# Two fused blocks on one core: attention weights normalised before they are turned, half the queries per level, another order at one join

## The reference

```python
PHASES = ["na", "ffn", "ple", "da", "ffn", "ple", "glu", "mix", "glu", "ple"]
```

```python
# gated linear recurrence, 4 heads of 128, in chunks of 64
scores = einsum('bhtd,bhsd,bhtsd->bhts', q_c, k_c, exp(b_t - b_s))   # t >= s
o = scores @ v_c + (q_c * exp(b)) @ state
# latent attention, 4 heads, blocks of 128 queries over the causal prefix
pr = softmax(where(mask, q @ k.T * scale, -inf))
o_mla = pr @ v
h = h + concatenate([rms_norm(o_hg) * silu(hg), o_mla]) @ w_out
```

## Time and profile before

| what | value |
|---|---|
| median of 3 runs | 1193.83 us (1193.71 to 1195.09) |
| the profiled execution | 1193.79 us, its span 1191.9 us |
| TensorE matmuls busy | 1179.1 us, 99% of the span, 6915 records |
| TensorE weight loads busy | 1028.1 us, 86% |
| VectorE busy | 933.1 us, 78% |
| ScalarE busy | 665.0 us, 56% |
| GpSimd busy | 139.0 us, 12% |
| mean granted clock of TensorE | 0.998 of full speed |
| DMA | 215.83 MB, 181 GB/s on the mean |

### The profile page before, as it was taken

How to read it: one execution, slowest core, us unless ns; L and a number is a source line. 1 busy time by engine, 2 the same in 40 slices (tenths; PEclk the granted TensorE clock), 3 DMA queues, 4 the chain that set the end, 5 groups by cost and what they waited for, 6 DMA issues and landing times.

```text
span 1191.9 us, 17766 instructions
## 1 busy us (share of the span) xinstructions
PE 1179.1 (99%) x6915; PEld 1028.1 (86%) x6915; DVE 933.1 (78%) x1270; ACT 665.0 (56%) x1059; POOL 139.0 (12%) x265
## 2 busy tenths in 40 slices
PE   8999999999999999999999999999999999999997
PEld 7998988888889989888888988888898888888886
DVE  6866898898777689989888898766776878766765
ACT  6756644444867786544446745444586664444445
POOL 5300600000300011000003100000206410000002
PEclk9999999999999999999999999999999999999999
DMA  9758376655544345665555575556455147556540
GB/s 297 223 156 269 124 244 207 210 179 178 190 139 148 129 163 195 212 205 185 182 173 179 184 230 189 189 187 203 136 191 177 44 161 228 176 197 204 185 142 36
DMA packets 151671, 215.83 MB, mean 181 GB/s; under 512 B 7002, under 2 KB 116956, under 8 KB 151588
## 3 DMA queue, kind: packets, MB, share of 16 engines
q1 hardware_dynamic: 148124, 207.46, 53.1%
q0 software_dynamic: 1760, 3.94, 1.3%
q10 hardware_dynamic: 1704, 3.28, 0.9%
HBM read 213.60 MB, written 1.06 MB: 180 GB/s over the span
## 4 chain that ended last, share of the span: by engine, by line
PE 93%; DVE 3%; ACT 1%; DMA 1%; issue 1%; POOL 0%; SPq 0%; POOLq 0%; ACTq 0%; DVEq 0%
PE work L2491 25%; PE work L2494 13%; PE acc L2072 10%; PE acc L2073 10%; PE acc L2074 10%; PE work L2072 5%; PE work L2073 5%; PE work L2074 5%; PE work L2094 1%; PE work L2480 1%; PE work L2468 1%; DVE w_lo L1357 1%; PE work L2482 1%; PE work L2619 1%; PE acc L2129 1%; PE acc L2270 1%
## 5 line engine op out<-in xcount | busy, mean ns | idle before, releaser
L1357 DVE TENSOR_TENSOR w_lo<-raw,w_hi 128x2048 fp32r<-128x2048 f32 (+1 forms) x192 | 436.0, 2277 | 51.5 <-ACT w_hi L752 51.5
L752 ACT ACTIVATE w_hi<-raw 128x2048 fp32r<-128x2048 f32 (+1 forms) x192 | 363.5, 1899 | 69.0 <-PE work L2494 59.4
L2491 PE MATMUL work<-hT_both,w_hi 128*128 128x512 f32 x1280 | 318.8, 391 | 0.0
L2491 PEld LDWEIGHTS work<-hT_both,w_hi 128*128 128x128 f32 x1280 | 234.8, 188 | 45.1
L2494 PEld LDWEIGHTS work<-hT_both,w_lo 128*128 128x128 f32 x1280 | 174.6, 190 | 12.5
L2494 PE MATMUL work<-hT_both,w_lo 128*128 128x256 f32 x1280 | 178.5, 282 | 0.0
L2072 PE MATMUL acc<-w_hi,aux_hi 128*128 128x512 f32 x400 | 158.0, 395 | 0.0
L2073 PE MATMUL acc<-w_lo,aux_hi 128*128 128x512 f32 x400 | 156.7, 392 | 0.0
L2074 PE MATMUL acc<-w_hi,aux_lo 128*128 128x512 f32 x400 | 155.8, 390 | 0.0
L1131 ACT ACTIVATE aux_hi<-Z 128x256 fp32r<-128x256 f32 x88 | 36.9, 419 | 195.4 <-DVE Z L1780 107.4
L1751 DVE TENSOR_REDUCE Z<-work 128x256 f32<-128x512 f32 x88 | 60.6, 689 | 89.5 <-PE work L2494 87.8
(11 more groups left out here) (283 smaller groups left out, 1740.2 us busy)
## 6 DMA issues: line engine op xcount, KB each, us to landing
raw<-in_ffn_w_in SPq DMA_DIRECT2D x44, 1024.0 KB, 5.1
raw<-in_ffn_w_out SPq DMA_DIRECT2D x22, 1024.0 KB, 5.1
raw<-in_w_gate SPq DMA_DIRECT2D x22, 1024.0 KB, 5.3
raw<-in_w_up SPq DMA_DIRECT2D x22, 1024.0 KB, 5.3
raw<-in_w_down SPq DMA_DIRECT2D x22, 1024.0 KB, 4.9
raw<-in_da_w_qkv SPq DMA_DIRECT2D x12, 1024.0 KB, 5.3
raw<-in_na_w_qkv SPq DMA_DIRECT2D x10, 1024.0 KB, 7.3
raw<-in_ple_w_gate SPq DMA_DIRECT2D x8, 1024.0 KB, 5.2
```

What stands on the lines that cost most here:

```text
L752: act.activation(w_hi[:, n % RING, 0:size], raw[:, n % RAW, 0:size], ACT.Copy).then_inc(hi_done, 1)
L1357: dve.tensor_tensor(w_lo[:, n % RING, 0:size], raw[:, n % RAW, 0:size], w_hi[:, n % RING, 0:size].bitcast(F32), ALU.subtract).then_inc(lo_ ...
L2491: pe.matmul(b.rearrange("p (e s) -> p e s", e=2), v[0][:, k, cols(c % 2)], hT_both[:, k, :, :], start=k == 0, stop=False)
```

## The change

It has three parts.

1. **Normalised weights, moving over resting values.** VectorE multiplies the exponentials by the reciprocal of their row sums before TensorE turns them (`normalised7`, with a semaphore of its own, `w7_ready`). In `outputs` the values are now the stationary operand and the turned weights the moving one, in two matmuls of 256 and 128 columns, so the result has queries along the free axis, as `late_piece` needs it. The stage `omla` with its eight transposes is gone. ScalarE and VectorE split each head's result directly (`output7` on both).
2. **Order in the mixer.** `gate_piece(1, 0)` stands directly after `gate_piece(0, 0)`, ahead of `weights(2)`. ScalarE's queue has `exps7(3)`, `output7(0)` and `output7(1)` ahead of `weights_turned7(2)`, and `output7(2)`, the slab and `output7(3)` between `decay(1)` and `decay(2)`. In levels 1 to 4 the moving operand holds only the 64 queries of the late halves, and `gather` writes only those.
3. **The join of phases 2 and 3.** TensorE's `turn_x(3, 0)` stands between the two halves of the last gate piece, `turn_x(3, 1)` ahead of the last block of `value_rows(3, 0, 1, 0)`. ScalarE and VectorE take their slab earlier, and their splits, sums and additions are interleaved in another order.

```diff
@@ plan @@
-                stage(f"V7.{u}", 1)
-            stage("omla", 2, (0, 1))
+                stage(f"V7.{u}", 1, (0,))
@@ ScalarE, gated_end, ph == 2 @@
                     gates(2, 1)
+                    feed(b + 6)
                     pre(3, 0)
-                    feed(b + 6)
                     gates(2, 2)
                     gates(2, 3)
-                    tile_parts(3, 0, range(4))
+                    tile_parts(3, 0, range(2))
+                    pre(3, 1, (0,))
+                    tile_parts(3, 0, range(2, 4))
+                    pre(3, 1, (1,))
                     gates(2, 4)
                     tile_parts(3, 0, range(4, 6))
-                    pre(3, 1, (0, 1))
+                    pre(3, 1, (2,))
                     tile_parts(3, 0, range(6, 8))
-                    pre(3, 1, (2,))
                     feed(b + 7)
                     tile_parts(3, 1)
@@ ScalarE, mixer @@
+            def output7(u):
+                g = G[f"V7.{u}"]
+                full(act, g)
+                split(aux_hi[:, u, :], backwards(bank(g)[:, 0:S]))
...
                 exps7(2)
+                exps7(3)
+                output7(0)
+                output7(1)
                 weights_turned7(2)
-                exps7(3)
                 weights_turned7(3)
                 decay(1)
+                output7(2)
                 feed(b + 15)
+                output7(3)
                 decay(2)
-                for t in range(T):
-                    full(act, G["omla"] + t)
-                    split(aux_hi[:, :, t * P:(t + 1) * P], backwards(bank(G["omla"] + t, 4)))
                 decay(3)
@@ VectorE, gated_end, ph == 2 @@
                     add_gated(2, 1)
+                    feed(b + 6)
                     normed(3, 0)
-                    feed(b + 6)
-                    tile_parts(3, 0, range(4))
                     add_gated(2, 2)
                     add_gated(2, 3)
-                    tile_parts(3, 0, range(4, 6))
+                    tile_parts(3, 0, range(4))
                     add_gated(2, 4)
-                    tile_parts(3, 0, range(6, 8))
+                    tile_parts(3, 0, range(4, 8))
                     normed(3, 1)
@@ VectorE, mixer @@
-            def output7(u):
+            def normalised7(u):
                 dve.wait_ge(exp_done, exps_before(7) + 2 * (u + 1))
                 link(dve.reciprocal(rinv[:, u % 4, 0:2], rsum[:, u % 4, 0:2]))
...
+                    tile = sc7[:, u, seen[a]]
+                    ins = dve.tensor_scalar(tile, tile, rinv[:, u % 4, a:a + 1], None, ALU.mult)
+                ins.then_inc(w7_ready, 1)
...
+            def output7(u):
+                split(aux_lo[:, u, :], backwards(bank(G[f"V7.{u}"])[:, 0:S]), aux_hi[:, u, :], H[f"V7.{u}"])
...
+                        n, r = P // (2 * LEVELS[i]), LEVELS[i]
+                        m = lmask[:, i, r:P]
+                        to = A[:, 4 * q:4 * q + 4, r:P]
+                        dve.copy_predicated(bass.AP(to.tensor, to.offset, [to.ap[0], [P, 4], [2 * r, n], [1, r]]),
+                                            bass.AP(m.tensor, m.offset, [m.ap[0], [0, 4], [2 * r, n], [1, r]]),
...
                 scores7(1)
+                normalised7(0)
+                normalised7(1)
                 keyed(0)
                 feed(b + 14)
                 scores7(2)
                 scores7(3)
+                normalised7(2)
+                normalised7(3)
                 output7(0)
                 output7(1)
...
                 gather(0)
+                keyed(1)
                 output7(2)
-                keyed(1)
                 output7(3)
                 keyed(2)
                 gather(1)
-                for t in range(T):
-                    tile = slice(t * P, (t + 1) * P)
-                    split(aux_lo[:, :, tile], backwards(bank(G["omla"] + t, 4)), aux_hi[:, :, tile], H["omla"] - 1 + t)
@@ TensorE @@
-                        if ph + 1 not in UNSCALED:
+                        if ph + 1 not in UNSCALED and ph != 2:
                             turn_x(ph + 1, 0)
                         pe.wait_ge(sig_done, 5 * ple_index(ph) + 3)
                     for kh in range(2):
+                        if ph == 2 and j == 1 and kh == 1:
+                            turn_x(3, 0)
...
                 value_rows(3, 0, 0, 0)
-                value_rows(3, 0, 1, 0)
+                value_rows(3, 0, 1, 0, range(3))
                 turn_x(3, 1)
+                value_rows(3, 0, 1, 0, range(3, 4))
...
-                    for a, k in ((0, 0), (0, 1), (1, 0)):
-                        ins = pe.matmul(d[:, cols(a)], pts7[:, u % 2, cols(2 * a + k)], vm[:, k, cols(u)],
-                                        start=k == 0, stop=k == 1 - a)
-                    ins.then_inc(bank_full[g % WORK], 1)
+                    pe.matmul(d[:, 0:S], vm[:, 0, cols(u)], pts7[:, u % 2, P:3 * P], start=True, stop=False)
+                    pe.matmul(d[:, 0:P], vm[:, 1, cols(u)], pts7[:, u % 2, 0:P], start=False, stop=True)\
+                        .then_inc(bank_full[g % WORK], 1)
...
+                                if 0 < i < QUAD:
+                                    late = q[:, 2 * j + h, cols(t)].rearrange("p (b e r) -> p b e r", e=2, r=LEVELS[i])
+                                    ins = pe.matmul(d[:, cols(2 * h + t, 64)].rearrange("p (b r) -> p b r", r=LEVELS[i]),
+                                                    k[:, 2 * j + h, cols(t)], late[:, :, 1, :], start=True, stop=True)
...
                 gate_piece(0, 0)
+                gate_piece(1, 0)
                 weights(2)
                 level(0)
                 weights(3)
                 outputs(2)
-                gate_piece(1, 0)
                 outputs(3)
                 level(1)
-                evacuated(pe, G["V7.3"])
-                for t in range(T):
-                    turn(G["omla"] + t, [xn[:, t, cols(4 + i)] for i in range(4)])
                 gate_piece(0, 1)
```

More of the change, by code:

```diff
@@ L1709, in scores7 @@
                 ins.then_inc(max_done, 1)
-            def output7(u):
-                g = G[f"V7.{u}"]
+            def normalised7(u):
                 dve.wait_ge(exp_done, exps_before(7) + 2 * (u + 1))
                 link(dve.reciprocal(rinv[:, u % 4, 0:2], rsum[:, u % 4, 0:2]))
-                full(dve, g)
-                col = u * VD + HGW
                 for a in range(2):
-                    ins = dve.tensor_scalar(xn[:, 1 - a, col:col + VD], bank(g)[:, a * VD:(a + 1) * VD],
-                                            rinv[:, u % 4, a:a + 1], None, ALU.mult)
-                ins.then_inc(bank_free[g % WORK], 1)
+                    tile = sc7[:, u, seen[a]]
[3 more added lines that the diff above has]
+                split(aux_lo[:, u, :], backwards(bank(G[f"V7.{u}"])[:, 0:S]), aux_hi[:, u, :], H[f"V7.{u}"])
             def bounds(c):
@@ L1880, in gather @@
                         evacuated(dve, G[f"lev{i - 1}"] + q)
-                        m = lmask[:, i, :]
-                        dve.copy_predicated(A[:, 4 * q:4 * q + 4, :], bass.AP(m.tensor, m.offset, [m.ap[0], [0, 4], [1, P]]),
-                                            bank(g, 4)).then_inc(bank_free[g % WORK], 1)
+                        if i == QUAD:
+                            m = lmask[:, i, :]
+                            dve.copy_predicated(A[:, 4 * q:4 * q + 4, :],
+                                                bass.AP(m.tensor, m.offset, [m.ap[0], [0, 4], [1, P]]),
+                                                bank(g, 4)).then_inc(bank_free[g % WORK], 1)
+                            continue
+                        n, r = P // (2 * LEVELS[i]), LEVELS[i]
[3 more added lines that the diff above has]
+                                            bass.AP(m.tensor, m.offset, [m.ap[0], [0, 4], [2 * r, n], [1, r]]),
+                                            bank(g)[:, 0:S].rearrange("p (a b r) -> p a b r", a=4, b=n))\
+                            .then_inc(bank_free[g % WORK], 1)
                 def query(i):
@@ L2169, in rows, with value_rows @@
                             ins.then_inc(used, 1)
-            def value_rows(ph, half, kh, t):
+            def value_rows(ph, half, kh, t, ks=range(4)):
                 v, g = slab(B[ph] + VALUE_SLABS[ph][half] + kh), G[f"v{ph}.{half}.{t}"]
                 b = open_bank(pe, g) if kh == 0 else work[:, g % WORK, :]
-                for k in range(4):
+                for k in ks:
                     if ph == 3 and half == 0:
@@ L2178, in value_rows @@
                                    kh == 0 and k == 0, kh == 1 and k == 3)
+                if ks[-1] < 3:
+                    return
                 if kh == 1:
@@ L2597, in weights @@
                 def weights(u):
-                    pe.wait_ge(exp_done, exps_before(7) + 2 * (u + 1))
-                    turn(G[f"T7.{u}"], [sc7[:, u, cols(i)] for i in range(3)])
+                    pe.wait_ge(w7_ready, u + 1)
```

(12 more changed lines are left out.)

2 lines of the change are left out of this document (1 added, 1 removed).

## The result

The changed kernel takes 1198.82 us in the median of 8 runs (1195.37 to 1201.76), the kernel before 1194.23 us (1193.71 to 1195.11) beside it. The ratio is 1.0038, with a 95% interval of 1.0030 to 1.0047: slower, by more than the 0.2% that the measurement tells. I had forecast 1193.1 us, with 1190.2 to 1195.2 as range; the result lies outside, on the side to which I gave 0.08.

A forecast was written before the change was run, and what follows sets the result against it. TensorE, busy for 99% of the span, was taken to bound the kernel. The join's -1.2 us and the mixer's +0.5 summed to -0.7, from 1193.83 us to a forecast of 1193.1, range 1190.2 to 1195.2.

The forecast's parts named there:

- the side to which I gave 0.08: Whole kernel: slower than the kernel before by over 0.2%, chance 0.08.
- the idle that I put in front of `level(1)`: Mixer: with `gate_piece(1, 0)` moved, `level(1)` starts 1.55 us late, at 928.7, and TensorE idles about 1.8 us.
- That chain: Mixer, `weights(3)` to `level(1)`: copy of T7.3, `decay(1)`, `keyed(1)`, then TensorE; 0.64 + 0.39 + 1.17 + 1.30 + 0.06 = 3.56 us.
- +0.5: Mixer as a whole: ends 0.5 us late, with bounds of +1.2 and -2.0 us.
- the durations below are at one level: Whole kernel: mean granted clock 0.998 of full speed (2.4 GHz), so all durations were taken at one level.
- my slower rival: Levels 1 to 4: strided moving operand reads slowly; 50 ns more per record turns the sum to +2.4 us; chance 0.08.
- The levels: Mixer, levels 1 to 4: halving moving columns to 64 gains 0, as the 128-column load sets the pace; 1.70 us per level.
- The rival of shorter levels: Levels 1 to 4: 64 moving columns save up to 2.55 us, giving 1190.5 us; chance 0.26.
- The transposes: Mixer: the eight `omla` transposes go, which cost 0.79 us.
- `level(1)` (0.24): Mixer: `level(1)` takes 1.70 us instead of 1.94, since it no longer waits for the copy of V7.3.
- the scalings of heads 0 and 1 find room: Mixer, VectorE: normalising heads 0 and 1 fits between the exponentials and `weights(0)`, with about 1 us to spare.
- The join: Phases 2 to 3: -1.2 us (0.48 + 0.68), bounds -0.6 and -1.7; rival of no gain gives 1194.3 us, chance 0.08.

The follow-up runs named there:

- the wait filled: The changed kernel with 12 identity matmuls ahead of `outputs(3)`, into a bank no longer read: 1195.44 us, ratio 1.0011 to the kernel before.
- split-ahead run: The changed kernel with `output7(2)` ahead of `decay(1)` on ScalarE and ahead of `keyed(1)` on VectorE: 1197.80 us, ratio 1.0023 to the kernel before.
- half queries alone: The kernel before with only levels 1 to 4 and their `gather` halved to 64 moving columns: 1194.26 us, ratio 1.0002.
- the splits earlier: Changed kernel, `gate_piece(1, 0)` back between `outputs(2)` and `outputs(3)`, `fall(2)` waiting for VectorE's four normalised heads, `output7(0)` to `output7(2)` earlier: 1193.07 us; again 1193.05.
- the piece put back: The changed kernel with `gate_piece(1, 0)` again between `outputs(2)` and `outputs(3)`: 1194.99 us, ratio 1.0008 to the kernel before.
- the join alone: The kernel before with only the new order at the join of phases 2 and 3, mixer untouched: 1193.63 us, ratio 0.9997.
- half-load kernel: The piece put back, with 64 stationary columns too in levels 1 to 4, leaving out each tile's later 64 keys: one run, 1195.45 us.
- the root free: The splits earlier, with VectorE's slab in the join behind `normed(3, 0)` instead of ahead of it: 1193.96 us, ratio 0.9998 to the kernel before.

## Why the prediction was wrong

**The step that failed** is the idle that I put in front of `level(1)`, "of which TensorE idles about 1.8, since `outputs(3)` ends near 926.8". I took `outputs(3)` as waiting for nothing but the copy of T7.3. It also opens the bank of V7.2, and in the new order both readers of V7.2 stand behind the chain that I had just worked out. That chain was sized well: from `weights(3)` to the end of `keyed(1)` I had 3.50 us, and VectorE turned to the next instruction 3.42 after (925.57 to 928.99). But what followed it was a split of 0.42 and `outputs(3)`, not `level(1)`. This turned 1.8 us of idle into 2.77. The run with the wait filled shows the mixer with this wait and at full clock: from `gate_piece(0, 0)` to `level(QUAD)` 30.18 us, +1.68 where I had +0.5.

**The larger part** is the sentence that "the durations below are at one level". I read the clock's mean of 0.998 as a property of the kernel. It is one of a TensorE that, once started, stands still for at most 0.94 us at a time, and I put a standstill of 1.8 us into the very schedule that I costed. The filled wait gives back 3.0 us in the medians; 4.7 are read in the profiled run, which is the slowest of the eight. In the split-ahead run an idle as long as I had forecast, in two parts, cost 3.4 us of clock in the profiled execution, and the mean clock of six of its nine runs is below 0.998. I had no rival in which an idle costs more than its own length; my slower rival was a mechanism that does not exist here.

**The levels** came out as forecast: no gain from 64 moving columns, 1.70 us each, shown by two experiments from both sides (moving halved: 1.70; stationary halved too: 1.07). With 128 stationary columns 0.106 us per record agrees with the rule of the Trainium skill that I had cited ("TensorE: Matmul & The Clock Gate", section "LDWEIGHTS (loading the stationary operand)"). With 64 columns the same rule gives 53 ns, an estimate from that page, and the runs show 58 (level 0) and 67. The rival of shorter levels and the one of slower strided reading both fell, the latter within 0.03 us per level: the levels start 4.56 apart where it was 4.53. These 0.03 lie in the pieces between the levels, and the half queries alone have them too.

**The transposes** (0.79) and `level(1)` (0.24) were right, and seen as such where no wait covers them, in the run with the splits earlier. So was the price of nothing for the two `outputs` matmuls. That the scalings of heads 0 and 1 find room held where ScalarE's slab ahead of the exponentials was in time, and cost 0.5 us in the profiled execution, where it was not. For head 2 I priced nothing, and it took 2.57 us beside `fall(2)`: I had counted 8 scalings for 8, and not that the new ones read SBUF. Here the moved gate piece hid it. The move of the piece thus covered two waits (0.96 and 0.87 in the kernel with the piece put back), and made one of 2.77 with a fall of the clock.

**The join** gave 0.45 us, not 1.2, and lies outside my bounds (from -0.6 on). The step: "VectorE's slab (2.3 us, like every slab) moves ahead too, into its wait for the root". The root does not go on while that slab runs, so the wait is not used but put behind it. In the join alone `normed` ends at 335.25, where I had 334.0. From there on TensorE is 0.6 to 0.8 us later than I had it (k = 0 at 337.79 for 337.16, the first columns of phase 3 at 351.42 for 350.6), and the rest of the reasoning holds: the turn of the second tile no longer waits (the 0.50 of the earlier trace rows is gone).

The Trainium skill has this ("SBUF — State Buffer", section "🔬 SBUF: two separate sides"): VectorE and GpSimd share a port pair of SBUF. A GpSimd instruction and one of VectorE that uses two ports, or has both its inputs in SBUF while the other reads SBUF too, shut each other out: the first to start holds the pair to its end. The rows agree in both directions, 2.19 us of GpSimd beside the slab and 0.22 without it, 2.69 us of VectorE beside `fall(2)` and 0.98 when that waits. They agree too in that the scalings of the kernel before, with their tensor in PSUM, took 0.61 us beside the same subtraction.

**In sum**: forecast -0.7. The join gave -0.45, the transposes, `level(1)` and the old idle -1.22, the new idle +2.77, the clock +4.7, the levels +0.1: +5.9 in the profiled execution. Its span is 6.8 longer. Of the rest 0.6 lies between the two places, most of it the late slab with the scalings of heads 0 and 1. Another 0.3 comes ahead of the join, where no kernel here differs from the one before; there the traces scatter by 1.2 us (the join starts at 329.97 to 331.13). The median is 4.6 longer.

**What stays open.** Why the clock falls in one run of the same kernel and not in the next was not settled: the piece put back has idles of 0.96 and 0.87 us and kept the clock in its profiled run, while the half-load kernel has 0.96 and 0.86 and lost it. The kernel with the piece put back keeps 0.998 or more in nine of eleven runs, the split ahead, with 1.02 and 0.93, in three of nine. Nor is the length of an idle enough to tell: the kernel with the root free stands still for 1.14 and then 0.86 us at the join, and it kept the clock there. What the join would give with a slab that costs VectorE nothing was not tried.

## What to carry to other kernels

When a wait is moved or made, ask not only who is late, but which bank the next instruction opens and where both of that bank's readers now stand in their queues; the order of reads is part of the chain. Where TensorE has been busy for 99% of the time, price a new idle of two to three us as more than its length: idle and clock together cost up to 2.7 times the idle here (2.77 + 4.7, 1.95 + 3.4), though not in every run, and useless matmuls in it paid. Before moving an operation of VectorE beside one of GpSimd "into a wait", look at what GpSimd does in that wait, and whether the operation reads SBUF or PSUM.

## What the runs showed of the hardware

- The granted clock fell from 1.00 to 0.50 near the end of an idle of 2.77 us in the profiled execution; five of the other seven runs have the same low mean. The work behind it took 1.41 + 3.28 + 5.24 us at 0.50, and 0.65 + 1.70 + 2.86 at 1.00. It also fell after two idles of 1.02 and 0.93 us, and in one run after 0.96 and 0.86. With matmuls of the identity in the wait it did not fall in any of 11 runs.
- A GpSimd instruction on one column took 2.19 us beside a VectorE `TENSOR_TENSOR` with both inputs in SBUF, and 0.22 without. Two VectorE `TENSOR_SCALAR` on 128 x 256 in SBUF took 2.69 us beside a GpSimd subtraction, and 0.55 without; two on 128 x 128 from PSUM took 0.61 beside one.
- An f32 matmul of 128 stationary columns costs 0.106 us per record with 128 moving columns and with 64. With 64 of both it is 0.067 (0.058 in level 0).
